# Two-layer encoder trunk: twelve of the 22 gate and up tiles of each feed-forward block by seven half-size products, the fourth weight sum on GpSimd

## The reference

```
D_MODEL = 1024; SEQ = 512; D_FF = 2816; FFN_RES = 0.5

def rmsnorm(x, g):
    xf = x.astype(jnp.float32)
    y = xf * lax.rsqrt(jnp.mean(xf * xf, axis=-1, keepdims=True) + EPS)
    return (y * g.astype(jnp.float32)).astype(x.dtype)

def swiglu(x, w_gate, w_up, w_down):
    return (jax.nn.silu(x @ w_gate) * (x @ w_up)) @ w_down

for layer in range(DEPTH):
    x = x + FFN_RES * swiglu(rmsnorm(x, ffn1_norm[layer]), ffn1_w_gate[layer], ffn1_w_up[layer], ffn1_w_down[layer])
    h = rmsnorm(x, mix_norm[layer])
    ...
    x = x + FFN_RES * swiglu(rmsnorm(x, ffn2_norm[layer]), ffn2_w_gate[layer], ffn2_w_up[layer], ffn2_w_down[layer])
```

## Time and profile before

| | us |
|---|---|
| median of 3 runs | 1889.01 |
| profiled execution | 1889.06 |
| span of its instructions | 1887.3 |
| TensorE busy | 1865.3 (99%) |
| VectorE busy | 841.8 (45%) |
| ScalarE busy | 656.8 (35%) |
| GpSimd busy | 365.9 (19%) |

### The profile page before, as it was taken

One profiled execution on the slowest core, in us unless ns is written; L12 is line 12 of the kernel. 1 busy time (PEld: TensorE's weight loads), 2 busy tenths in 40 slices (PEclk: granted clock), 3 DMA queues, 4 the chain that ended last, 5 costly groups with the idle time before them and its releaser, 6 DMA issues.

```text
span 1887.3 us, 22491 instructions
## 1 busy us (share of the span) xinstructions
PE 1865.3 (99%) x8333; PEld 1523.6 (81%) x8333; DVE 841.8 (45%) x969; ACT 656.8 (35%) x851; POOL 365.9 (19%) x317
## 2 busy tenths in 40 slices
PE   8999999999989999999999999999999999999999
PEld 6888888887568888888888888888888888888887
DVE  5433433377776534333434344333455444344321
ACT  5333332246866433332224333322312343333221
POOL 3111111139883211110111111101113121111000
PEclk9999999999999999999999999999999999999999
DMA  5333343332102333333323333433233333333331
GB/s 158 92 98 100 93 119 92 86 82 76 33 7 85 100 100 92 97 108 108 92 82 89 100 100 89 121 93 99 78 96 94 101 91 99 100 91 106 109 113 38
DMA packets 341404, 174.86 MB, mean 93 GB/s; under 512 B 6304, under 2 KB 340332, under 8 KB 341356
## 3 DMA queue, kind: packets, MB, share of 16 engines
q1 hardware_dynamic: 337100, 172.12, 31.6%
q10 hardware_dynamic: 4256, 2.11, 0.4%
HBM read 172.10 MB, written 2.10 MB: 92 GB/s over the span
## 4 chain that ended last, share of the span: by engine, by line
PE 91%; POOL 3%; DVE 2%; ACT 2%; issue 1%; DMA 0%; SPq 0%; ACTq 0%; POOLq 0%
PE bank L1290 30%; PE bank L1291 30%; PE bank L1292 30%; POOL conv L499 2%; DVE w_lo L950 1%; POOL probs_a L594 0%; ACT w_hi L637 0%; DVE conv L986 0%; DMA x_rows<-in_x 0%; PE bank L1353 0%; DVE pt_lo L1189 0%; PE bank L1538 0%; PE bank L1488 0%; ACT tap_prod L770 0%; DVE neg_max L1196 0%
## 5 line engine op out<-in xcount | busy, mean ns | idle before, releaser
L950 DVE TENSOR_TENSOR w_lo<-raw,w_hi 128x1024 fp32r<-128x1024 f32 (+2 forms) x308 | 407.1, 1323 | 734.9 <-ACT w_hi L637 734.5
L1290 PE MATMUL bank<-xg_hi,w_hi 128*128 128x512 f32 x1728 | 677.0, 392 | 3.3 <-DVE w_lo L950 2.7
L1292 PE MATMUL bank<-xg_hi,w_lo 128*128 128x512 f32 x1728 | 672.9, 389 | 0.0
L1291 PE MATMUL bank<-xg_lo,w_hi 128*128 128x512 f32 x1728 | 672.8, 389 | 0.0
L637 ACT ACTIVATE w_hi<-raw 128x1024 fp32r<-128x1024 f32 (+2 forms) x308 | 340.1, 1104 | 767.6 <-PE bank L1292 767.4
L1290 PEld LDWEIGHTS bank<-xg_hi,w_hi 128*128 128x128 f32 x1728 | 324.6, 188 | 78.0 <-issue 5.2
L1291 PEld LDWEIGHTS bank<-xg_lo,w_hi 128*128 128x128 f32 x1728 | 324.7, 188 | 68.4 <-issue 1.4
L1292 PEld LDWEIGHTS bank<-xg_hi,w_lo 128*128 128x128 f32 x1728 | 324.6, 188 | 67.3
L516 POOL TENSOR_TENSOR scaled<-acted,rstd 128x512 f32<-128x512 f32 x92 | 118.8, 1291 | 860.8 <-ACT acted L688 849.3
L1290 PE MATMUL bank<-h_hi,w_hi 128*128 128x512 f32 x704 | 274.4, 390 | 0.0
L1292 PE MATMUL bank<-h_hi,w_lo 128*128 128x512 f32 x704 | 274.0, 389 | 0.0
(11 more groups left out here) (192 smaller groups left out, 1127.9 us busy)
## 6 DMA issues: line engine op xcount, KB each, us to landing
raw<-in_ffn_w_gate SPq DMA_DIRECT2D x88, 512.0 KB, 3.8
raw<-in_ffn_w_up SPq DMA_DIRECT2D x88, 512.0 KB, 3.8
raw<-in_ffn_w_down SPq DMA_DIRECT2D x64, 704.0 KB, 4.5
raw<-in_od_w_in SPq DMA_DIRECT2D x24, 512.0 KB, 3.8
raw<-in_ev_w_in SPq DMA_DIRECT2D x20, 512.0 KB, 3.8
raw<-in_ev_w_out SPq DMA_DIRECT2D x16, 256.0 KB, 2.8
raw<-in_od_w_out SPq DMA_DIRECT2D x8, 512.0 KB, 3.8
x_rows<-in_x SPq DMA_DIRECT2D x4, 512.0 KB, 6.8
```

Of the source, the lines that this page charges most:

```text
L950: dve.tensor_tensor(w_lo[:, u % 2, c0:c0 + n], raw[:, u % 4, 0:n], raws(w_hi[:, u % 2, c0:c0 + n]), ALU.subtract).then_inc(wlo_ready, 1)
L1290: pe.matmul(dst, a[0], b[0], start=start, stop=False)
L1291: pe.matmul(dst, a[0], b[1], start=False, stop=False)
L1292: return pe.matmul(dst, a[1], b[0], start=False, stop=stop)
```

## The change

In each of the four feed-forward blocks tiles 4 to 15 (`FOLD0` to `FOLD1`) are computed by Strassen's scheme in its form with seven products. The gate tile and the up tile of one f are seen together as a 2x2 block matrix of weights: rows split into the first and the last four k-tiles, columns into gate and up (`b11` gate first half, `b21` gate second half, `b12` up first half, `b22` up second half). The input is split the same way, first and last four k-tiles, first and last 256 rows of time. Seven products `p1` to `p7`, each 4 k-tiles times 3 matmuls of 256 columns, take the place of two units of 24 matmuls of 512 columns. The k-tiles of the halves, their sums and the weight sums `t1` to `t4` have to be formed:

- The input must be normalised for this, since sums over time columns mix different `rstd`. VectorE makes `xn` (8 of `normalise`), GpSimd the sums `s1`, `s2`, `s4`, `s3` (128x1024 each), ScalarE and VectorE the high and low halves of seven operands (`quad_high`, `quad_low`, 128x1024 each). All that is in the first two groups (tiles 0 to 3). Since these operands lie where `h` will go, GpSimd then copies four of them over `xg` (8 copies of 128x1024), and `p1` of tile 6 waits for these (`quad_moved`).
- The weight sums: `t1`, `t3`, `t2` by `mix` on VectorE (128x512 each), `t4` on GpSimd, in place over `t2`.
- The weights' high and low halves lie in a ring of `RING = 2 * SLOT // FOLD_W = 2816 // 512 = 5` places of 128x512; the high half of product n waits for product n-5.
- Partial results: ScalarE copies three 128x256 pieces from PSUM to SBUF (`keep`), VectorE adds them (`second_up`, `join_gate`), and makes `hid` in two halves of 256. `one` on GpSimd is gone from these tiles and from tiles 16 to 21 (`tail`), since the input is normalised.

```diff
+FOLD0, FOLD1 = 4, 16
...
+    def fold_order(name, f):
+        n = f - FOLD0
+        if name in ("p1", "p7", "p6", "p4"):
+            first = ("p1", "p7", "p6", "p4").index(name)
+            return first if n == 0 else 4 + 7 * (n - 1) + 2 * first
+        last = ("p5", "p2", "p3").index(name)
+        return 4 + 7 * n + (2 * last + 1 if n < FOLDS - 1 else last)
...
@@ gpsimd, gates @@
                 one(0, 0)
                 one(1, 1)
+                if ph.gate == "silu":
...
+                    pool.wait_ge(xn_ready, 12 * e + KD)
+                    pool.tensor_tensor(s1, c, d, ALU.add).then_inc(sum_ready, 1)
+                    one(2, 0)
+                    pool.wait_ge(sum_ready, 4 * e + 1)
+                    pool.tensor_tensor(s2, s1, a, ALU.subtract).then_inc(sum_ready, 1)
+                    pool.wait_ge(sum_ready, 4 * e + 2)
+                    pool.tensor_tensor(s4, b, s2, ALU.subtract).then_inc(sum_ready, 1)
+                    pool.tensor_tensor(s3, a, c, ALU.subtract).then_inc(sum_ready, 1)
+                    one(3, 1)
...
+                    for f in range(FOLD0, FOLD1):
+                        pool.wait_ge(mix_ready, mix_count(ph, "t2", f))
+                        wait_block(pool, ph, "t2", f, wlo_ready, slo_ready)
+                        pool.tensor_tensor(block_raw("t4", f), block_raw("b21", f), block_raw("t2", f), ALU.subtract)\
+                            .then_inc(mix4_ready, 1)
+                        for name in {FOLD0: ("a11", "a22"), FOLD0 + 1: ("s1", "a12")}.get(f, ()):
+                            ks, ts = XG_PART[name]
+                            for n, whole in enumerate((xg_hi, xg_lo)):
+                                pool.tensor_copy(whole[:, ks, ts], raws(quad[name][n][:, :, :])).then_inc(quad_moved, 1)
...
@@ scalar @@
+            def block_high(ph, block, f):
...
+                if n < RING:
+                    act.wait_ge(unit_done, ph.unit0 + 2 * FOLD0 - (1 if n < 2 else 0))
+                else:
+                    wait_product(act, ph, n - RING)
...
+                act.activation(ring_hi[:, n % RING, :], block_raw(block, f), ACT.Copy).then_inc(done, 1)
...
+            def folded(ph):
+                f = FOLD0
+                block_high(ph, "t4", f)
+                block_high(ph, "b11", f + 1)
+                keep(ph, f, "p1")
...
+                for f in range(FOLD0, FOLD1 - 1):
+                    block_high(ph, "t2", f + 1)
+                    if f > FOLD0:
+                        hidden_high(ph, f - 1)
+                    block_high(ph, "b22", f)
+                    keep(ph, f + 1, "p1")
+                    block_high(ph, "t4", f + 1)
+                    if f + 2 < FOLD1:
+                        block_high(ph, "b11", f + 2)
+                    keep(ph, f + 1, "p7")
+                    block_high(ph, "t1", f + 1)
+                    if f + 2 < FOLD1:
+                        block_high(ph, "t3", f + 2)
+                    gate_silu(ph, f)
+                    keep(ph, f + 1, "p6")
+                    block_high(ph, "b21", f + 1)
...
@@ vector @@
+            def mix(ph, name, f):
+                if name == "t1":
+                    arrived(dve, ph, f, 0)
+                    arrived(dve, ph, f, 1)
+                if name != "t1":
+                    dve.wait_ge(mix_ready, mix_count(ph, "t1", f))
+                if name != "t3" and f > FOLD0:
+                    wait_block(dve, ph, {"t1": "t1", "t2": "t4"}[name], f - 1, wlo_ready, slo_ready)
+                one, other = {"t1": ("b12", "b11"), "t3": ("b22", "b12"), "t2": ("b22", "t1")}[name]
+                dve.tensor_tensor(block_raw(name, f), block_raw(one, f), block_raw(other, f), ALU.subtract)\
+                    .then_inc(mix_ready, 1)
...
+            def folded(ph):
...
+                for f in range(FOLD0, FOLD1 - 1):
+                    block_low(ph, "t2", f + 1)
+                    if f > FOLD0:
+                        hidden_low(ph, f - 1)
+                    block_low(ph, "b22", f)
+                    block_low(ph, "t4", f + 1)
+                    second_up(ph, f)
+                    if f + 2 < FOLD1:
+                        block_low(ph, "b11", f + 2)
+                    block_low(ph, "t1", f + 1)
+                    if f + 2 < FOLD1:
+                        mix(ph, "t1", f + 2)
+                        mix(ph, "t3", f + 2)
+                    join_gate(ph, f)
+                    if f + 2 < FOLD1:
+                        mix(ph, "t2", f + 2)
+                        block_low(ph, "t3", f + 2)
+                    block_low(ph, "b21", f + 1)
+                    hidden(ph, f)
...
@@ tensor @@
+            def p1(ph, f):
+                if f == FOLD0:
+                    pe.wait_ge(quad_lo, 8 * ph.fold + 7)
+                if f == FOLD0 + 2:
+                    pe.wait_ge(quad_moved, 8 * (ph.fold + 1))
+                pe.wait_ge(pair_out, ph.pair0 + f - 1)
+                folded_product(ph, "p1", f, "a11", True, True)
...
+            def folded(ph):
...
+                for f in range(FOLD0, FOLD1 - 1):
+                    p1(ph, f + 1)
+                    p5(ph, f)
+                    p7_(ph, f + 1)
+                    p2(ph, f)
+                    p6(ph, f + 1)
+                    p3(ph, f)
+                    p4(ph, f + 1)
```

More of the change, by code:

```diff
@@ L630, in split_hi @@
                         act.wait_ge(unit_done, i - 3)
+                    elif ph.gate == "silu" and i - ph.unit0 == 2 * FOLD1:
+                        wait_product(act, ph, 7 * FOLDS - 3)
                     elif i >= 2:
@@ L669, in group @@
                         f, par = g * 2 + u // 2, u // 2
-                        if not (first and u in (1, 2)):
+                        if fold and g == 1:
+                            for name in ((), ("a11", "a22"), ("a12", "s1"), ("s2", "s4", "s3"))[u]:
+                                quad_high(ph, name)
+                        if fold and g == 1 and u == 2:
+                            block_high(ph, "b11", FOLD0)
+                            block_high(ph, "t3", FOLD0)
+                        elif fold and g == 1 and u == 3:
+                            block_high(ph, "t2", FOLD0)
+                        elif not (first and u in (1, 2)):
                             split_hi(ph, g, u + 2)
@@ L996, in pair, with tail @@
+            def tail(ph):
+                for f in range(FOLD1, KF):
+                    split_lo(ph, f // 2, f % 2 * 2 + 2)
+                    split_lo(ph, f // 2, f % 2 * 2 + 3)
+                    hidden(ph, f)
+                    hidden_low(ph, f)
             def pair(ph):
+                fold = ph.gate == "silu"
                 def group(g):
@@ L1000, in group @@
                         f, half = g * 2 + u // 2, u // 2
+                        if fold and g == 1:
+                            for name in ((), ("a11", "a22"), ("a12", "s1"), ("s2", "s4", "s3"))[u]:
+                                quad_low(ph, name)
+                        if fold and g == 1 and u == 2:
+                            for name in ("t1", "t3", "t2"):
+                                mix(ph, name, FOLD0)
                         if ph is A_GATE and not first and u == 0:
@@ L1026, in group @@
                                 .then_inc(gate_scaled, 1)
+                            if fold:
+                                for j in {(0, 2): (0, 1, 2), (1, 0): (5, 6, 7)}.get((g, u), ()):
+                                    normalise(ph, j)
                             if ph is A_GATE:
```

335 lines of the change are left out of this document (314 added, 21 removed).

## The result

The changed kernel takes 2091.7 us (median of 4 runs, 2090.1 to 2095.4) where the kernel before takes 1890.4 on the same chip: a ratio of 1.107 (95% interval 1.105 to 1.109). The forecast was 2045 us, range 1980 to 2100. One of the four runs of e1_busy (2779 us) and one of e3_order (4677 us) were slow runs, so the medians given for these two kernels are those of the other three.

What follows compares the result with a forecast made beforehand. The prediction took TensorE, busy 99%, to bound the kernel before. Per block 15.0 + 11.3 + 19.9 + 0.8 + 1.7 - 9.7 = 39.0 us, 156 in four, took the span from 1887.3 to 2043.3; with 1.8 around it 2045 us, range 1980 to 2100.

Steps and rivals of the forecast that it cites:

- What TensorE saves: Changed tiles: 84 matmuls of 0.120 us, 10.08 us in place of 10.88; 9.7 us saved per block, 38.7 in all.
- The steady tile: p1 of tiles 7 to 15: VectorE's order makes a 12.3 us loop, TensorE waiting 2.2; 19.9 us per block.
- The load of the up tile: Steady tile: nearly a second bound, landing at 7.0 us where sum t1 wants it at 7.36.
- The first groups: Tiles 0 to 3: VectorE and GpSimd exclude each other; eighth unit 4.4 us late, p1 of tile 4 15.0 late.
- The first two changed tiles: p1(4) to p1(6): 27.1 us where eleven products take 15.8, so 11.3 us lost, with copies of 1.1 each.
- The rest: Block end: unit 32 waits 0.8 us for the restored operand quarter; other work lies beside TensorE, dropping `one` gains nothing.
- Clock: Behind the 5.7 us wait ahead of p1(6): one stretch of TensorE at half clock, 1.7 us lost per block.
- the fall in the loop: Rival, chance 0.10: the clock falls after each of the nine loop waits, 61 us more, 2106 us.
- The port matters less: Rival, chance 0.10: VectorE and GpSimd overlap in the first groups; 22.5 us per block, 90 in all, 1979 us.
- Faster: Rival, chance 0.06: TensorE stays the bound, tiles take 10.08 us and the first groups are hidden; 1850 us.

Runs made afterwards that it cites:

- e1_busy: The changed kernel with 18 unused 256-column matmuls on TensorE ahead of the wait of p1, from tile 7 on; 2050.5 us.
- e3_order: The changed kernel with its steady tile reordered: on VectorE join_gate and hidden come earlier, mix t2, low t3 and low b21 after hidden; 1984.8 us.
- after: The changed kernel itself, with seven products in tiles 4 to 15, against the kernel before; 2091.7 us.
- e2_t4: The changed kernel with the fourth weight sum of each tile on VectorE, behind the low half of t2, in place of GpSimd; 2097.3 us.
- e5_sums: The changed kernel with GpSimd's four whole input sums cut to their first column; 2066.0 us.
- e6_sumdve: The changed kernel with the four whole input sums on VectorE in place of GpSimd; 2079.1 us.
- e11_fill: e10_all with unused 256-column matmuls on TensorE, 48 ahead of p1 of tile 4 and 12 ahead of p1 of tile 6; 1959.7 us.
- e8_swap: e3_order with low b22 ahead of h_lo on VectorE and high b22 ahead of h_hi on ScalarE; 1976.0 us.
- e10_all: The changed kernel with steady tile reordered, low b22 ahead of h_lo, whole sums on VectorE, and copies spread over four tiles; 1956.3 us.

## Why the prediction was right in its sign and 47 us low

Measured, four blocks, from the starts of p1 in the trace of after, beside the forecast's terms times four:

| Term | Forecast | Measured | From |
|---|---|---|---|
| p1 of tile 4 late | 60 | 62 | 17.2 in the first block, 15.0 in each of the others |
| p1(4) to p1(6) | 45 | 41 | 26.1 to 26.3 less 15.84: 32.5 of waits, 8.9 of matmuls at a clock of 0.5 |
| nine periods, the loop | 80 | 88 | 36 x (12.53 - 10.08) |
| nine periods, the clock | 7 | 47 | 497.8 less 36 x 12.53 |
| end of the block | 3 | 5 | ten products from p1(15) on: 14.8, 14.8, 16.3 and 16.2 us, at 0.120 a matmul 14.4 |
| TensorE's gain | -39 | -39 | 0.120 us per matmul |
| Sum | 156 | 204 | blocks longer by 50.9, 50.8, 50.4 and 52.6 us; spans differ by 202.9 |

- **What TensorE saves**: right, by the row of attention.
- **The steady tile**: right in mechanism and within 2% in the period (12.53 for 12.29). e3_order shows that it is VectorE's order: the wait shrinks from 2.35 to mostly 0.62 us when three rows leave the place between the joined gate and `hid`. e2_t4 confirms that GpSimd's t4 costs nothing there. The load of the up tile, named as nearly a second bound, closes only some of the rounds of e3_order.
- **The first groups**: right to 0.1 us in three blocks, 2.2 too low in the first. The eighth unit came 4.7 us late for 4.4; that the total agrees to a tenth is partly luck, as three of the four sums took 2.8 to 3.3 us where 2.4 were taken. The port's turns, which the Trainium skill (SBUF — State Buffer, Who interferes with whom) states and which were read in one place of the trace of before, are all over the first groups of after, and e5_sums and e6_sumdve show how much of the loss is theirs: 6.8 us of 15.0 go with the sums, and 2.6 when VectorE computes them.
- **The first two changed tiles**: 10.3 for 11.3 us, again in part by luck. TensorE's waits were 8.1 us a block where the forecast had 11.3 of waits alone (p6 of tile 4 waited 0.8 to 1.6 us, not 3.2), and 2.2 us are matmuls at a clock of 0.5, which it did not count there. The copy was estimated at 1.1 us and took 1.04 alone. The estimate of 0.85 from the Trainium skill (GPSIMD Engine Reference, Engine selection) lay below it; this case's row decides.
- **The rest**: the wait of 0.8 us ahead of unit 32 did not come; its first matmul starts 0.12 us after the last product in every block. What the end lost instead is mostly a fall of the clock behind p1 of tile 15, in two of the four blocks.
- **The step that failed** is the term "Clock", 1.7 us per block, placed behind the wait of 5.7 us ahead of p1(6) only. It measured 11.7 us a block: 2.1 in the period behind that wait, near what was forecast, and 9.6 behind the other waits of the loop, which the sum put at nothing; the granted clock of the execution was 0.956 where near 0.97 was named. The forecast's own rows spoke of it: a fall after 2.33 us of idleness, none after 1.59, and the loop waits 2.2. And a fall after a wait is not seen once in the trace of before, as the forecast has it, but twice. The second, of 6.8 us, comes in attention behind idle times of 0.9 to 1.2 us close to each other (windows as above):

```profile
523.67:527.08 3.41, 1.83 (x18) 1.42 (x18) 2.18 (x7) 3.41 (x11) 3.41 (x4) 1.00 0.00 0
527.08:530.49 3.41, 3.09 (x16) 1.88 (x14) 2.57 (x7) 2.29 (x8) 3.41 (x4) 0.50 0.02 5
```

  I put the fall in the loop as a rival at 0.10 and it was what happened, in 30 of 36 periods. Its price was also nearly right: 61 us more by the rival, 40 more by the trace, since a fall in a steady tile cost mostly 1.4 to 1.5 us and not every tile had one. The repeated wait was nearer to the one after which the clock fell than to the one after which it stayed, and I should have given it the greater chance.
- **The port matters less** fell by the traces: rows of VectorE at two to three times their length beside GpSimd. **Faster** fell by every row of 512 columns.

What stays open: why some tiles escaped a fall under the same wait. Of the 36 waits of 2.35 us (p1 of tiles 7 to 15) 28 were followed by one. The 8 that were not share one thing: the fall before them, of 3.4 us, had begun no later than its own p1 and up to 0.3 us ahead of it, while behind a fall that began later the next tile had one too. No run tries a recurring pause between 1.3 and 2.35 us. Single ones stand in the traces of the repaired kernels, without a clear border: a fall came after 1.95 and 2.09 us (e11_fill), 2.17 (e3_order), 2.18 (e8_swap) and 2.28 (e10_all), none after 1.82 (e10_all), 2.00 (e8_swap) and 2.20 (e3_order).

## What to carry to other kernels

Fewer matmul columns are a gain only if every engine's row for a tile still closes its loop within the shorter tile: write the row out, and look for what stands between the value that TensorE waits for and the one that makes it, as the same instructions in another order were worth 107 us here. A wait that recurs in each tile is to be costed twice, once as itself and once as the clock that it may take along; unused matmuls in a part of the wait tell the two apart. A method that needs sums and copies before it starts pays for them per block, so compare this fixed cost with the gain of all tiles of the block first: 12 us late in the best version, against 9.7.
